# Scores of an RWKV-7 head pair in quadrants, and three steps around them in another order

## The chip, the core and the metric

The kernel runs on one core of a Trainium2 chip. The metric is the device time of one execution in microseconds. Three runs of the kernel before gave 1024.72 us as median (1024.06 to 1024.76).

Engines are called PE (TensorE, matmuls), DVE (VectorE), ACT (ScalarE), POOL (GpSimd) and SP (SyncE, which issues most loads). Each works through its own list of instructions in order; semaphores make one wait for another.

## The reference

One layer of a hybrid model on 512 tokens of width 1024: an RWKV-7 time mix with 16 heads of 64, a window attention, gates, a projection, and a feed-forward part with a short convolution. The change lies in the time mix:

```python
def step(S, inp):
    r_t, w_t, k_t, v_t, aa_t, bb_t = inp
    sa = jnp.einsum('bhvk,bhk->bhv', S, aa_t)
    S = S * w_t[:, :, None, :] + sa[..., None] * bb_t[:, :, None, :] + v_t[..., None] * k_t[:, :, None, :]
    y_t = jnp.einsum('bhvk,bhk->bhv', S, r_t)
    return S, y_t
...
y = (y - mean) * lax.rsqrt(var + GN_EPS)
y = y.reshape(B, T, RWKV_DIM) * lnx_w.astype(f32) + lnx_b.astype(f32)
bonus = jnp.sum(rh * kh * r_k.astype(f32), axis=-1, keepdims=True) * vh
y = (y + bonus.reshape(B, T, RWKV_DIM)) * g.astype(f32)
```

## The kernel before

The 512 steps of the recurrence are done in NT = 4 chunks of C = 128 tokens. Heads are taken in PAIRS = 8 pairs; the two heads of a pair lie on partitions 0 to 63 and 64 to 127. For each pair n, DVE prepares four operands: bp and kp (keys, all 512 tokens) and, in the tile ar, a-tilde and r-tilde side by side (2 x 128 columns a chunk). From them the kernel makes, per chunk and head, two triangular score matrices of 128 keys by 2 x 128 tokens: gb from bp, gk from kp. A key counts only for later tokens (a-tilde's half: strictly later; r-tilde's half: also the same one). The mask `causal` says so, and what it masks stays at the zero that POOL wrote once (and gb's -1 on the diagonal).

The part of a pair on PE is scores(n), then invert(n), then scan(n):

- scores(n, d), with d = n - 1. It waits for ops_ready (bp, kp and ar are there). Line L2291 makes 16 products: weights are 64 x 128 of bp or kp (one head, one chunk), 256 columns of ar move. Each fills half a PSUM bank; SCORE_BANK = (0, 1, 2, 3, 4, 5, 0, 1) gives the bank of each of eight halves of work f, so that f = 6 and 7 use the banks of 0 and 1 again and wait for two masked copies (g_ready). Then norm_var(d), L2226: the sums for the variance of the previous pair and the bonus sums, in four strips of 32 columns. Then turnings (transposes, L2232 and L2277): z (the values), bp, kp, and for the previous pair yrow (its standard deviation) and ysq (its reciprocal spread out).
- invert(n): a triangular inverse in LEVELS = 7 levels. At level 0 PE multiplies n1 (gb's first half, rounded to fp16 by ACT; n2 is the remainder, made by POOL at L738) by the identity (L2355); DVE masks the result to yy (L1597); from level 1 on PE makes L2351, DVE masks v (L1597), PE makes L2374, DVE adds to yy (L1608), ACT copies transposes. xx is made by DVE at L1582 from n1.
- scan(n): four chunks in turn, state, output.

Between these small steps PE always has "fill" work: L2046 to L2048, three products of 512 columns for one step of an unrelated big projection. The tables FILL and FILL_FIRST say how many such steps stand at each place ("scores", "centred", "tokens", (level, "masks") and so on).

DVE masks with copy_predicated (L1532, function masked), eight times a pair, 512 elements a partition each: f = 0 to 3 give gb, 4 to 7 give gk. In front of each stands a tiny memset of carrier. In pairs 1 to 7 deviations(d) (reciprocal L1520 and spread L1507) stands between the sixth and the seventh, and value_tokens(n) (L1497, L1499: the values less their mean) behind the eighth. Before the masks DVE splits weights (L1357) and, in pairs 1 and 2, also shifts a tile (L1392).

POOL, for each pair n > 0: bonus_product (L745), a copy (L752), remainder(n) (n2, L738), bonus_back(n - 1) (L814 writes the bonus rows to HBM once the deviation is there, L817 reads them back to all partitions), key_norms_in (L808), and the product of bonus and value (L850), which DVE uses at level 4. POOL also clears gb and, later, gk (L829) once before pair 0; the semaphore `cleared` counts 1, 2, 3 for gb, gk and zp.

SP's loads and their order are not touched.

## Time and profile before

| | |
|---|---|
| median of 3 runs | 1024.72 us (1024.06 to 1024.76) |
| profiled execution | 1024.05 us, of which the span of the trace is 1022.3 us |
| PE busy | 1011.7 us, 99% |
| DVE busy | 738.1 us, 72% |
| ACT busy | 516.2 us, 50% |
| POOL busy | 224.4 us, 22% |
| granted clock of PE | 0.999 of full speed |

The scores of pair 0 start at 213.64 us of the span, those of pair 7 at 498.12 us. Times in the rows are microseconds from the span's start. In the timeline views a row merges equal instructions that follow each other: it gives the start of the first, the time from there to the end of the last, and their number. Ends of matmuls are modelled and overlap the next one's start, so starts are compared with starts. An fp32 product on PE is two matmul instructions in these views; a turning (transpose) is one.

### The profile page before, as it was taken

The numbers are of one execution on the slowest core, as the hardware profiler recorded it, in microseconds if no ns is written. First come the engines' busy times: TensorE is split into PE (matmuls) and PEld (weight loads), VectorE is DVE, ScalarE is ACT, GpSimd is POOL, SyncE is SP. The second block draws the span as 40 slices with busy tenths as digits, with TensorE's granted clock in tenths as the row PEclk, the third lists the DMA queues.
The fourth block names the chain that finished last, engine by engine and source line by source line (L and its number), as shares of the span: only waits on it lengthen the run. The fifth ranks groups of instructions, "written<-read, shape, count | busy, mean of one in ns | idle before, by whom it ended". The sixth has DMA issues, their size and how long they took to land.

```text
span 1022.3 us, 18746 instructions
## 1 busy us (share of the span) xinstructions
PE 1011.7 (99%) x7106; PEld 806.3 (79%) x7106; DVE 738.1 (72%) x1233; ACT 516.2 (50%) x869; POOL 224.4 (22%) x298
## 2 busy tenths in 40 slices
PE   8999999999999999999999999999999999999997
PEld 7888888777777777777777888888888888888886
DVE  5224667788988888888877565367767777789786
ACT  6435756844435445345453322264455444467744
POOL 7642355330221422413210554000000000000000
PEclk9999999999999999999999999999999999999999
DMA  6874456331303313214255867613233333337662
GB/s 187 233 236 153 132 191 215 94 76 43 86 25 74 86 63 87 61 60 120 93 164 153 238 234 258 198 40 103 85 102 92 95 100 103 92 114 226 203 189 113
DMA packets 161291, 133.25 MB, mean 130 GB/s; under 512 B 32729, under 2 KB 137735, under 8 KB 161223
## 3 DMA queue, kind: packets, MB, share of 16 engines
q1 hardware_dynamic: 147687, 88.41, 29.7%
q0 software_dynamic: 13520, 43.90, 13.9%
q8 instruction: 47, 0.77, 0.3%
q14 instruction: 21, 0.17, 0.0%
q10 hardware_dynamic: 16, 0.00, 0.0%
HBM read 111.83 MB, written 20.45 MB: 129 GB/s over the span
## 4 chain that ended last, share of the span: by engine, by line
PE 94%; DVE 2%; DMA 1%; issue 1%; ACT 1%; POOL 0%; SPq 0%; DVEq 0%; POOLq 0%; ACTq 0%
PE ps L2090 14%; PE ps L2093 14%; PE ps L2092 14%; PE ps L2046 6%; PE ps L2048 5%; PE ps L2047 5%; PE ps L2677 3%; PE ps L2678 3%; PE ps L2679 3%; PE ps L2291 3%; PE ps L2425 2%; PE ps L2232 2%; PE ps L2613 1%; PE ps L2611 1%; PE ps L2612 1%; PE ps L2374 1%
## 5 line engine op out<-in xcount | busy, mean ns | idle before, releaser
L1357 DVE TENSOR_TENSOR wlo<-raw,whi 128x1024 fp32r<-128x1024 f32 x106 | 140.1, 1322 | 125.9 <-ACT whi L893 108.0
L893 ACT ACTIVATE whi<-raw 128x1024 fp32r<-128x1024 f32 x116 | 122.6, 1057 | 127.0 <-PE ps L2093 116.0
L2090 PE MATMUL ps<-xnh,whi 128*128 128x512 f32 x336 | 130.7, 389 | 0.0
L2092 PE MATMUL ps<-xnl,whi 128*128 128x512 f32 x336 | 130.7, 389 | 0.0
L2093 PE MATMUL ps<-xnh,wlo 128*128 128x512 f32 x336 | 130.7, 389 | 0.0
L2046 PE MATMUL ps<-xh,whi 128*128 128x512 f32 x192 | 89.5, 466 | 0.0
L2090 PE MATMUL ps<-xh,whi 128*128 128x512 f32 x224 | 88.3, 394 | 0.0
L2092 PE MATMUL ps<-xl,whi 128*128 128x512 f32 x224 | 87.3, 390 | 0.0
L2093 PE MATMUL ps<-xh,wlo 128*128 128x512 f32 x224 | 87.2, 389 | 0.0
L2048 PE MATMUL ps<-xh,wlo 128*128 128x512 f32 x192 | 76.1, 396 | 0.0
L2047 PE MATMUL ps<-xl,whi 128*128 128x512 f32 x192 | 75.3, 392 | 0.0
L2090 PEld LDWEIGHTS ps<-xnh,whi 128*128 128x128 f32 x336 | 63.1, 188 | 13.2
L2092 PEld LDWEIGHTS ps<-xnl,whi 128*128 128x128 f32 x336 | 63.1, 188 | 13.2
L2093 PEld LDWEIGHTS ps<-xnh,wlo 128*128 128x128 f32 x336 | 63.1, 188 | 13.0
L1093 ACT ACTIVATE xx<-ps 128x256 f16<-128x256 f32 x96 | 32.1, 381 | 69.1 <-PE ps L2331 68.3
L2090 PEld LDWEIGHTS ps<-xh,whi 128*128 128x128 f32 x224 | 42.0, 188 | 10.1 <-issue 0.8
L2093 PEld LDWEIGHTS ps<-xh,wlo 128*128 128x128 f32 x224 | 42.1, 188 | 8.9
L2092 PEld LDWEIGHTS ps<-xl,whi 128*128 128x128 f32 x224 | 42.1, 188 | 8.4
L1879 DVE TENSOR_TENSOR sq<-ps,rs 128x512 f32<-128x512 f32 x44 | 30.4, 691 | 23.5 <-PE ps L2093 18.5
L745 POOL TENSOR_TENSOR z<-z,kmod 128x512 f32<-128x512 f32 x8 | 16.2, 2025 | 126.2 <-DVE kp L1488 126.2
L2048 PEld LDWEIGHTS ps<-xh,wlo 128*128 128x128 f32 x192 | 36.0, 188 | 8.3
L1608 DVE TENSOR_TENSOR yy<-ps,yy 128x256 f16<-128x256 f32 x96 | 36.2, 419 | 8.6 <-PE ps L2374 8.3
(430 smaller groups left out, 2454.6 us busy)
## 6 DMA issues: line engine op xcount, KB each, us to landing
raw<-in_w_in SPq DMA_DIRECT2D x108, 256.0 KB, 3.3
raw<-in_w_up SPq DMA_DIRECT2D x88, 256.0 KB, 3.0
wrow<-in_w_down POOLq DMA_DIRECT2D x22, 512.0 KB, 5.1
raw<-weight_scratch SPq DMA_DIRECT2D x44, 256.0 KB, 3.4
raw<-in_w_down SPq DMA_DIRECT2D x32, 256.0 KB, 2.9
weight_scratch<-wrow POOLq DMA_DIRECT2D x11, 512.0 KB, 3.1
gates_scratch<-gst POOLq DMA_DIRECT2D x16, 256.0 KB, 3.2
raw<-in_w_proj_b SPq DMA_DIRECT2D x16, 256.0 KB, 4.2
```

The source lines that it names most:

```text
L893: act.activation(flat(whi[:, hb]), flat(raw[:, b]), ACT.Copy).then_inc(w_hi, 1)
L1093: act.activation(dst, src, ACT.Copy).then_inc(x_ready, 1)
L1357: dve.tensor_tensor(flat(lo[:, hb]), flat(raw[:, b]), flat(hi[:, hb]).bitcast(F32), ALU.subtract).then_inc(w_lo, 1)
L1608: dve.tensor_tensor(yg, low_half(ps[2 * g][:, :], lv), yg, ALU.add)\
L2046: pe.matmul(o, whi[:, hb, k, :], self.hi(k), start=k == 0, stop=False)
L2047: pe.matmul(o, whi[:, hb, k, :], self.lo(k), start=False, stop=False)
L2048: ins = pe.matmul(o, wlo[:, hb, k, :], self.hi(k), start=False, stop=k == KT - 1)
L2090: pe.matmul(ps[bank][:, :], whi[:, hb, k, :], hi(k), start=first and k == 0, stop=False)
L2092: pe.matmul(ps[bank][:, :], whi[:, hb, k, :], lo(k), start=False, stop=False)
L2093: ins = pe.matmul(ps[bank][:, :], wlo[:, hb, k, :], hi(k), start=False, stop=last and k == kn - 1)
L2291: ins = pe.matmul(ps[SCORE_BANK[f + h]][:, (j - j0) * 2 * C: (j - j0 + 1) * 2 * C], src[hs, j * C:(j + 1) * C], ar[hs, 1 - n % 2, j, :], s ...
L2677: pe.matmul(o, h_hi, hi[:, cols], start=start, stop=False)
```

## The change

It does four things.

1. Scores in quadrants. A chunk's 128 keys are split: the first 64 keys are multiplied with the first 64 tokens ("early", 64 x 64 weights, 2 x 64 = 128 columns, both chunks of a couple into the two partition halves of a bank), and all 128 keys with the last 64 tokens ("late", 128 columns). The last 64 keys with the first 64 tokens, all masked, are not computed. Early work goes to banks 2 and 3, late work of bp to 0 and 1, of kp to 4 and 5, so no bank is used twice and PE's wait inside the scores is gone.
2. The masked copies follow: four early ones on 64 partitions, each for gb and gk together (gb and gk become the two halves of a tile gg), two late ones for gb, two for gk. All four early ones wait for g_ps 4; in pair 0 they also wait for cleared 2, where the first copy waited for cleared 1. Memsets go from eight to five.
3. On DVE value_tokens and deviations stand between the sixth and seventh copy. On PE turned_var stands behind bp's turning, and turning ysq (deviations) and the wait for n1_ready stand behind the "tokens" fill of invert. Waits of g_ready change from 3, 4 and 8 to 2, 4 and 6, and ACT's copy to n1 waits for 6 instead of 4.
4. On POOL bonus_back stands before remainder, and remainder also waits for x_start, which DVE gives when xx is made.

```diff
--- before.py
+++ after.py
@@ -52,7 +52,8 @@
 RKV_TILES = 17
 RKV_LOOP = RKV_TILES - 1
 FILL_BANK = (7, 4, 7)
-SCORE_BANK = (0, 1, 2, 3, 4, 5, 0, 1)
+EARLY_BANK = (2, 3)
+LATE_BANK = ((0, 1), (4, 5))
 WARM = 24
 HALF_EXP = float(-0.5 * np.exp(-0.5))
 NEG = -1e30
@@ -273,11 +274,12 @@
         brow = take("brow", [P, P])
         lih = take("lih", [P, T], F32R)
         take = taker(KVR, PREP)
-        gb = take("gb", [P, NT, 2, 2 * C])
+        gg = take("gg", [P, NT, 2, 2, 2, C])
+        gb, gk = (gg[:, 2 * i:2 * i + 2].rearrange("p x e h q t -> p (x e) h (q t)")
+                  for i in range(2))
         gst = take("gst", [P, 2, T])
         xx = take("xx", [P, NT, 2, C], F16)
         ysb = take("ysb", [P, T])
-        gk = take("gk", [P, NT, 2, 2 * C])
         rkcols = take("rkcols", [P, P // NT])
 
 
@@ -735,6 +737,7 @@
 
             def remainder(n):
                 pool.wait_ge(n1_ready, n + 1)
+                pool.wait_ge(x_start, n + 1)
                 pool.tensor_tensor(n2[:, :, :, :], gb[:, :, :, 0:C], n1[:, :, :, :], ALU.subtract)\
                     .then_inc(n2_ready, 1)
 
@@ -841,8 +844,8 @@
                 if 3 * n - 1 >= FILL_V:
                     gate_out(3 * n - 1 - FILL_V)
                 odd_columns(n)
+                bonus_back(n - 1)
                 remainder(n)
-                bonus_back(n - 1)
                 if n < PAIRS - 1:
                     pool.wait_ge(rstd_ps, n)
                     key_norms_in(n + 1)
@@ -1069,7 +1072,7 @@
                 act.activation(flat(ktok), ps[1][:, :], ACT.Copy).then_inc(tok_ready, 1)
 
             def score_copy(n):
-                act.wait_ge(g_ready, n * 8 + 4)
+                act.wait_ge(g_ready, n * 8 + 6)
                 act.activation(n1[:, :, :, :], gb[:, :, :, 0:C], ACT.Copy).then_inc(n1_ready, 1)
 
             def hi_part(dst, src, i):
@@ -1520,19 +1523,42 @@
                 chain(dve.reciprocal(by_token(ystd[:, :]), by_token(ps[6][:, P:2 * P])))
                 spread(ysq, ystd).then_inc(vex_ready, 1)
 
-            def masked(n, f):
-
-                j0, h = (f % 4) // 2 * 2, f % 2
-                dst = (gb, gk)[f // 4][:, j0:j0 + 2, h, :]
+            def two_parts(t, ts):
+                return t.rearrange("p (q t) -> p q t", q=2)[:, :, ts]
+
+            def predicated(dst, mask, scores, f=None):
+                if f is not None:
+                    dve.memset(carrier[:, f:f + 1], 0.0)
+                dve.copy_predicated(dst, mask.bitcast(U32).unsqueeze(1)
+                                    .to_broadcast([mask.shape[0], NT, 2, C // 2]), scores)\
+                    .then_inc(g_ready, 1)
+
+            def late_masked(n, i, h):
+                f = 4 + 2 * i + h
                 if n == 0:
-                    dve.wait_ge(cleared, 1 + f // 4)
+                    dve.wait_ge(cleared, 1 + i)
                 dve.wait_ge(g_ps, n * 8 + f + 1)
-
-                dve.memset(carrier[:, f:f + 1], 0.0)
-                dve.copy_predicated(dst, causal[:, :].bitcast(U32).unsqueeze(1)
-                                    .to_broadcast([P, 2, 2 * C]),
-                                    ps[SCORE_BANK[f]][:, :].rearrange("p (j t) -> p j t", j=2))\
-                    .then_inc(g_ready, 1)
+                predicated((gb, gk)[i][:, :, h, :].rearrange("p j (q t) -> p j q t", q=2)
+                           [:, :, :, C // 2:], two_parts(causal[:, :], slice(C // 2, C)),
+                           ps[LATE_BANK[i][h]][:, :].rearrange("p (j q t) -> p j q t", j=NT, q=2), f)
+
+            def early_masked(n, h, e):
+                if n == 0:
+                    dve.wait_ge(cleared, 2)
+                dve.wait_ge(g_ps, n * 8 + 4)
+                predicated(gg[0:HD, :, e, h, :, 0:C // 2],
+                           two_parts(causal[0:HD, :], slice(0, C // 2)),
+                           ps[EARLY_BANK[h]][e * HD:(e + 1) * HD, :]
+                           .rearrange("p (x q t) -> p x q t", x=NT, q=2),
+                           None if h or e else 0)
+
+            def masked(n, i):
+                if i == 0:
+                    for h in range(2):
+                        for e in range(2):
+                            early_masked(n, h, e)
+                for h in range(2):
+                    late_masked(n, i, h)
 
             def add_bonus(d):
                 dve.wait_ge(bonus_ps, 1)
@@ -1714,9 +1740,9 @@
                 piece()
             attention_copy(7)
             weights(n + 2)
-            for f in range(8):
-                masked(0, f)
+            masked(0, 0)
             value_tokens(0)
+            masked(0, 1)
             invert(0, None, True)
             for n in range(1, PAIRS):
                 key, rates, factor, modified, removed, a_tilde, r_tilde, b_hat, k_hat = prepare(n)
@@ -1725,12 +1751,10 @@
                              (2, "s"): [r_tilde], (3, "z"): [b_hat], (3, "u"): [k_hat]})
                 weights(N_FILL + 3 * n)
                 fill_low(3 * n - 1)
-                for f in range(6):
-                    masked(n, f)
+                masked(n, 0)
+                value_tokens(n)
                 deviations(n - 1)
-                for f in range(6, 8):
-                    masked(n, f)
-                value_tokens(n)
+                masked(n, 1)
                 invert(n, n - 1, n < PAIRS - 1)
 
             def gated_bonus(d):
@@ -2281,32 +2305,47 @@
                 pe.wait_ge(ops_ready, n + 1)
                 if n == 0:
                     pe.wait_ge(ps_free, N_FILL - 1)
-                for f in range(0, 8, 2):
-                    src, j0 = (bp, kp)[f // 4], f % 4
-                    if f == 6:
-                        pe.wait_ge(g_ready, n * 8 + 2)
-                    for j in range(j0, j0 + 2):
-                        for h in range(2):
-                            hs = slice(h * HD, (h + 1) * HD)
-                            ins = pe.matmul(ps[SCORE_BANK[f + h]][:, (j - j0) * 2 * C:
-                                                                  (j - j0 + 1) * 2 * C],
-                                            src[hs, j * C:(j + 1) * C], ar[hs, 1 - n % 2, j, :],
+                rows = [slice(h * HD, (h + 1) * HD) for h in range(2)]
+
+                def both(hs, j, ts):
+                    return ar[hs, 1 - n % 2, j, :].rearrange("p (q t) -> p q t", q=2)[:, :, ts]
+
+                def late(i):
+                    src = (bp, kp)[i]
+                    for j in range(NT):
+                        for h, hs in enumerate(rows):
+                            ins = pe.matmul(ps[LATE_BANK[i][h]][:, j * C:(j + 1) * C]
+                                            .rearrange("p (q t) -> p q t", q=2),
+                                            src[hs, j * C:(j + 1) * C], both(hs, j, slice(HD, C)),
                                             start=True, stop=True)
-                            if j > j0:
+                            if j == NT - 1:
                                 ins.then_inc(g_ps, 1)
+
+                for i, src in enumerate((bp, kp)):
+                    for jj in range(2):
+                        o = (2 * i + jj) * C
+                        for e in range(2):
+                            j = 2 * jj + e
+                            for h, hs in enumerate(rows):
+                                ins = pe.matmul(ps[EARLY_BANK[h]][e * HD:(e + 1) * HD, o:o + C]
+                                                .rearrange("p (q t) -> p q t", q=2),
+                                                src[hs, j * C:j * C + HD], both(hs, j, slice(0, HD)),
+                                                start=True, stop=True)
+                                if i and jj:
+                                    ins.then_inc(g_ps, 1)
+                late(0)
+                late(1)
                 if d is not None:
                     norm_var(d)
                 fill("scores")
-                if d is not None:
-                    turned_var(d)
-                pe.wait_ge(g_ready, n * 8 + 3)
+                pe.wait_ge(g_ready, n * 8 + 2)
                 turned(2, z[:, n + 16, :]).then_inc(tok_ps, 1)
                 pe.wait_ge(g_ready, n * 8 + 4)
                 turned(3, bp).then_inc(tok_ps, 1)
                 if d is not None:
-                    deviations(d)
+                    turned_var(d)
                 fill("centred")
-                pe.wait_ge(g_ready, n * 8 + 8)
+                pe.wait_ge(g_ready, n * 8 + 6)
                 turned(1, kp).then_inc(tok_ps, 1)
 
             halves = [slice(h * HD, (h + 1) * HD) for h in range(2)]
@@ -2331,13 +2370,15 @@
                         ins = pe.matmul(o, yy[:, j, h, :], i, start=True, stop=True)
                     return ins
 
-                pe.wait_ge(n1_ready, n + 1)
                 for lv in range(LEVELS):
 
                     if lv == 4 and d is not None:
                         gate(d)
                     if lv == 0:
                         fill("tokens")
+                        if d is not None:
+                            deviations(d)
+                        pe.wait_ge(n1_ready, n + 1)
                     for g in range(2):
                         if lv == 0:
                             if g == 1:
```

PE in pair 1, before. The place begins at the scores and ends at the first matmuls of the inversion; fill work (L2046 to L2048) and the variance sums (L2226) are left out:

```order
L2291 MATMUL ps<-ar,bp 128x256 x8
L2291 MATMUL ps<-ar,kp 128x256 x8
...
L2277 MATMUL ps<-ident,yrow 128x128
L2232 MATMUL ps<-ident,z 128x128 x4
L2232 MATMUL ps<-ident,bp 128x128 x4
L2232 MATMUL ps<-ident,ysq 128x128 x4
...
L2232 MATMUL ps<-ident,kp 128x128 x4
...
L2355 MATMUL ps<-ident,n_95 128x64 x8
```

PE at the same place, after. L2330 are the early products, L2317 the late ones, L2256 and L2301 the turnings, L2396 the inversion's first matmuls:

```order
L2330 MATMUL ps<-ar,bp 64x128 x8
L2330 MATMUL ps<-ar,kp 64x128 x8
L2317 MATMUL ps<-ar,bp 128x128 x8
L2317 MATMUL ps<-ar,kp 128x128 x8
...
L2256 MATMUL ps<-ident,z 128x128 x4
L2256 MATMUL ps<-ident,bp 128x128 x4
L2301 MATMUL ps<-ident,yrow 128x128
...
L2256 MATMUL ps<-ident,kp 128x128 x4
...
L2256 MATMUL ps<-ident,ysq 128x128 x4
L2396 MATMUL ps<-ident,n_95 128x64 x8
```

Sixteen products of 256 columns have become 16 of 64 keys and 16 of 128 keys, each of 128 columns; yrow moved behind bp, and ysq from behind bp to behind kp.

DVE in pair 1, before, from the fifth masked copy to xx (the four before it are alike):

```order
L1532 COPY_PREDICATED gk<-causal,ps 128x2x256
L1531 MEMSET carrier 128x1
L1532 COPY_PREDICATED gk<-causal,ps 128x2x256
L1520 RECIPROCAL ystd<-ps 128x8
L1507 COPY ysq<-ystd 128x512
L1531 MEMSET carrier 128x1
L1532 COPY_PREDICATED gk<-causal,ps 128x2x256
L1531 MEMSET carrier 128x1
L1532 COPY_PREDICATED gk<-causal,ps 128x2x256
L1497 TENSOR_REDUCE vsum<-ps 128x8
L1499 SCALAR_TENSOR_TENSOR vp<-vsum,ps 128x512
L1582 TENSOR_TENSOR xx<-n_95,first_level 128x1024
```

DVE in pair 1, after, from the four early copies to the seventh; L1500 and L1502 are value_tokens, L1523 and L1510 deviations:

```order
L1532 COPY_PREDICATED gg<-causal,ps 64x4x2x64 x4
L1531 MEMSET carrier 128x1
L1532 COPY_PREDICATED gg<-causal,ps 128x4x2x64
L1531 MEMSET carrier 128x1
L1532 COPY_PREDICATED gg<-causal,ps 128x4x2x64
L1500 TENSOR_REDUCE vsum<-ps 128x8
L1502 SCALAR_TENSOR_TENSOR vp<-vsum,ps 128x512
L1523 RECIPROCAL ystd<-ps 128x8
L1510 COPY ysq<-ystd 128x512
L1531 MEMSET carrier 128x1
L1532 COPY_PREDICATED gg<-causal,ps 128x4x2x64
```

value_tokens has moved from behind the eighth copy to behind the sixth, in front of deviations.

POOL in pair 1, before, and then after (L741 is remainder, L817 and L820 the bonus rows, L811 the key rows):

```order
L745 TENSOR_TENSOR z<-z,kmod 128x512
L752 COPY yy<-ident 128x512
L738 TENSOR_TENSOR n_97<-gb,n_95 128x1024
L814 DMA bonus_scratch<-brow 128x128
L817 DMA z<-bonus_scratch 64x4x128 x2
L808 DMA kqn<-key_scratch 64x4x128 x2
L850 TENSOR_TENSOR z<-z 128x512
```

```order
L748 TENSOR_TENSOR z<-z,kmod 128x512
L755 COPY yy<-ident 128x512
L817 DMA bonus_scratch<-brow 128x128
L820 DMA z<-bonus_scratch 64x4x128 x2
L741 TENSOR_TENSOR n_97<-gg,n_95 128x1024
L811 DMA kqn<-key_scratch 64x4x128 x2
L853 TENSOR_TENSOR z<-z 128x512
```

Here n2 has moved behind the bonus rows' three DMAs.

## Rows read from the trace of the kernel before

**Rows 1.** The page's part 1: busy us (share of the span) and instructions of each engine

```profile
PE 1011.7 (99%) x7106; PEld 806.3 (79%) x7106; DVE 738.1 (72%) x1233; ACT 516.2 (50%) x869; POOL 224.4 (22%) x298
```

**Rows 2.** PE in order of time, pair 7; start us, length us, engine, line, operation

```profile
498.12 2.00 PE L2291 MATMUL ps<-ar,bp 64*128 64x256 f32 x16
...
501.78 0.43 PE L2226 MATMUL ps<-ysq,meancols 128*32 128x128 f32 x8
502.03 0.40 PE L2226 MATMUL ps<-z,rkcols 128*32 128x128 f32 x8
...
503.71 0.60 PE L2232 MATMUL ps<-ident,bp 128*128 128x128 f32 x4
504.19 0.66 PE L2232 MATMUL ps<-ident,ysq 128*128 128x128 f32 x4
...
504.92 0.40 PE L2047 MATMUL ps<-xl,whi 128*128 128x512 f32 x1
505.16 0.40 PE L2048 MATMUL ps<-xh,wlo 128*128 128x512 f32 x1
505.52 0.66 PE L2232 MATMUL ps<-ident,kp 128*128 128x128 f32 x4
...
508.63 0.42 PE L2351 MATMUL ps<-yy,n 128*128 128x64 f16 x8
```

**Rows 3.** PE in order of time, pair 1

```profile
253.87 2.00 PE L2291 MATMUL ps<-ar,bp 64*128 64x256 f32 x16
...
257.82 0.42 PE L2226 MATMUL ps<-ysq,meancols 128*32 128x128 f32 x8
```

**Rows 4.** DVE in order of time, pair 7; in brackets idle time before and what ended it

```profile
499.30 0.74 DVE L1532 COPY_PREDICATED gb<-causal,ps 128x512 f32<-128x512 uint32 x1 [0.29 <-issue]
...
499.93 0.73 DVE L1532 COPY_PREDICATED gb<-causal,ps 128x512 f32<-128x512 uint32 x1
...
503.47 0.21 DVE L1520 RECIPROCAL ystd<-ps 128x8 f32<-128x8 f32 x1 [0.24 <-PE ps L2277]
...
505.36 0.68 DVE L1497 TENSOR_REDUCE vsum<-ps 128x8 f32<-128x512 f32 x1
...
506.67 0.68 DVE L1582 TENSOR_TENSOR xx<-n,first_level 128x1024 f16<-128x1024 f16 x1
507.27 0.77 DVE L1597 TENSOR_TENSOR yy<-ps,level_mask 128x256 f16<-128x256 f32 x2
```

**Rows 5.** PE in order of time, scores of an attention window

```profile
84.36 1.16 PE L2176 MATMUL ps<-kb,qc 64*128 64x128 f32 x16
85.45 0.50 PE L2090 MATMUL ps<-xh,whi 128*128 128x512 f32 x1
```

**Rows 6.** PE in order of time, pair 0

```profile
218.51 0.60 PE L2232 MATMUL ps<-ident,z 128*128 128x128 f32 x4
...
223.84 0.44 PE L2351 MATMUL ps<-yy,n 128*128 128x64 f16 x8
```

**Rows 7.** DVE in order of time, pair 0

```profile
215.24 0.73 DVE L1532 COPY_PREDICATED gb<-causal,ps 128x512 f32<-128x512 uint32 x1
...
221.67 1.49 DVE L1582 TENSOR_TENSOR xx<-n,first_level 128x1024 f16<-128x1024 f16 x1
```

**Rows 8.** POOL in order of time, pair 0

```profile
215.26 1.88 POOL L829 MEMSET gk<- 128x2048 f32 x1
...
220.43 2.17 POOL L738 TENSOR_TENSOR n<-gb,n 128x1024 f16<-128x1024 f32 x1
```

**Rows 9.** One line, L1597; lengths in ns min/median/max, first and last start us

```profile
L1597 DVE TENSOR_TENSOR v<-ps,level_mask x96: 414/418/425, 224.2 to 521.9; 128x256 f16<-128x256 f32 x96
```

**Rows 10.** POOL in order of time, pair 7

```profile
506.15 0.57 POOL L814 DMA_DIRECT2D bonus_scratch<-brow  x1
...
514.66 1.29 POOL L850 TENSOR_TENSOR z<-z 128x512 f32<-128x512 f32 x1 [4.08 <-DMA z<-bonus_scratch]
```

**Rows 11.** DVE in order of time, pair 7, inversion's level 2

```profile
512.96 0.68 DVE L1569 TENSOR_TENSOR wlo<-raw,whi 128x512 fp32r<-128x512 f32 x1
```

## The prediction

> **What bounds the kernel now.** I read the page first: TensorE (PE) is busy 99% of the span [rows 1]. A microsecond cut from PE's own instructions is therefore gained, as long as nothing that PE waits for comes later than PE then arrives. I then read PE in order of time in the last pair of heads (n = 7), by starts: an instruction counts as busy until its modelled end, so busy time hides short stalls. The score matmuls run from 498.12 to 501.78 us, 3.66 us for 32 matmul instructions of 256 columns (each fp32 product is two instructions). From their start to the first L2351, the level-1 matmuls of the inversion, it is 508.63 - 498.12 = 10.51 us [rows 2]. Pair 1 takes 257.82 - 253.87 = 3.95 us for the same scores, since its last quarter waits for the masked copy that frees bank 0 [rows 3]. Then VectorE (DVE) over the same stretch: the eight masked copies follow each other every 0.63 us, with one hole of 0.24 us before the reciprocal, and DVE starts the first yy at 507.27, 1.36 us before PE's L2351 [rows 4]. One yy takes about 0.4 us, half of the 0.77 us of the two. What is left of these 1.36 us decides how much of a PE saving arrives.
>
> **PE's scores, pairs 1 to 7.** Before: 16 products of 64x128 weights with 256 columns. The two heads use different row halves and overlap: 3.66 us for 16 pairs of instructions. After: 16 products of all 128 keys with 128 columns ("late"), and 16 of 64 keys with 128 columns ("early"), which sit in four quadrants of the array. The late form exists in the trace: kb,qc, 64*128 weights and 128 columns, takes 85.45 - 84.36 = 1.09 us for 16 instructions, getting in and out included [rows 5]. If getting in and out is 0.2 of that, the 32 late ones take 2 x 0.9 + 0.2 = 2.0 us. No 64x64 quadrant runs in before. Nearest is ysq,meancols, four column strips at once: 8 instructions of 128 columns in 502.03 - 501.78 = 0.25 us [rows 2]; the 32 early ones at that rate take 1.0 us. The other end is two at a time, as kb,qc: 1.8 us. I take 1.0, since both forms show different parts of the array overlapping. Between early and late the tiles change shape once more: 0.1 us, half of what I gave kb,qc. New total 3.1 us. That is 0.56 less in pairs 3 to 7, and 0.85 less in pairs 1 and 2, because no bank is used twice any more.
>
> **PE's turnings.** Turning ysq stands behind bp's, and PE arrives before its operand: bp's four take 0.48 us until ysq starts, and ysq's are 0.66 us long where bp's are 0.60; 0.1 us is waiting. kp's start 0.36 us behind the filler's last start, where filler instructions follow each other at 0.24, and are 0.66 long too: 0.2 us of waiting, for the eighth masked copy [rows 2]. After the change kp waits for the sixth copy and ysq stands a filler block behind kp, so both waits should go: 0.3 us. PE's saving is 0.87 us in each of pairs 3 to 7 and 1.15 in 1 and 2.
>
> **Does DVE arrive in time?** Its work stays: eight copies of 512 elements a partition (four of them on 64 partitions, which I count as no cheaper), three memsets fewer, and the hole of 0.24 us goes because value_tokens now fills it. Its first copy can start where it did: the early products are done 1.3 us after the scores' start, and DVE came 1.18 us after it, from the weights [rows 2, 4]. From 499.30: six copies 3.7 us; reciprocal, spread and two copies 505.36 - 503.47 = 1.9; reduce, subtraction and xx 507.27 - 505.36 = 1.9 [rows 4]. The first yy starts near 506.8 and is ready near 507.3. PE arrives at 508.63 - 0.87 = 507.76: 0.4 us of slack. In pairs 1 and 2 DVE has one operation more (L1392) in front of its copies, so there I expect hardly any slack, and count 1.1 instead of 1.15. n1 waits for six copies instead of four, which moves ACT's copy by the time of one or two of them, not past xx. PE's wait for vex_ready now stands in front of the inversion's first matmuls; by the same counting the spread ends near 505.2 and PE is there at 505.4: no stall, but little room.
>
> **Pair 0 loses.** An early copy writes both gb and gk, so DVE's first one now waits until POOL has cleared gk. POOL does that from 215.26 to 217.14; DVE's first copy started at 215.24 [rows 6 to 8]. So DVE starts 1.95 us later, and its second copy is ready near 217.2 + 0.63 + 0.74 = 218.6. PE came to z's turning at 218.51 and, with shorter scores, would come at about 217.6: 1.0 us of standing. Its next turning, bp's, waits for the fourth copy, ready near 219.85, where PE is at 219.05; it starts near 219.95. From z's start to L2351 it was 5.33 us before, with z's four turnings, 0.44 us, ahead of bp's; so L2351 comes at 219.95 + 4.9 = 224.9 instead of 223.84 [rows 6]: a loss of 1.1 us. If POOL's clearing were hidden it would be nothing; the other end is the whole 1.95.
>
> **POOL.** The bonus rows go out before n2 is made, and n2 now waits for x_start; it is needed only at the end of the inversion. In pair 0 xx took 1.49 us, with POOL's n2 (220.43, 2.17 us) beside it, and 0.60 elsewhere [rows 4, 7, 8]. That goes, but PE, later itself in this pair, gains nothing from it. The Trainium skill, page "SBUF — State Buffer", section "SBUF: two separate sides", says that a VectorE operation with two SBUF inputs and a GpSimd operation that reads SBUF lock each other out of a shared port for the whole instruction. By that rule xx waited for n2's end at 222.60, and the trace agrees: it ended at 223.16.
>
> **The sum.** Pairs 3 to 7: 5 x 0.87 = 4.35. Pairs 1 and 2: 2 x 1.1 = 2.2. Pair 0: -1.1. Together 5.4 us less. The profiled execution took 1024.05 us (span 1022.3), so 1018.6; the median of the runs stands 0.7 above it, so 1019.3 us. After the pairs the same instructions follow behind the same PE, so nothing should give it back.
>
> **Rivals.**
> DVE becomes the bound of the stretch. For it: slack 0.4 us or less, and copies of 64-element runs that before does not have. Against: L1597's masks take 0.41 to 0.43 us in all 96 cases, at runs of every power of two from 1 to 64 [rows 9]. If every copy took 0.1 us more, eight of them are 0.8 us; less the slack, the pairs gain about 0.45: 7 x 0.45 - 1.1 = 2.0, 1022.7 us.
> Quadrants overlap only in part. With two at a time the early part takes 1.8 us: the scores come to 3.9, 0.25 more than now in pairs 3 to 7 against 0.3 from the waits that go; pairs 1 and 2 gain 0.35; pair 0 loses 1.1: 1024.4 us. Half way between, 1.4 us, each pair loses 0.4 of its gain: 1022.1 us. The Trainium skill, "TensorE: Matmul & The Clock Gate", section "Measured speedup vs the span model", has 3.07-fold for four row tiles, short of four; by it as an estimate the time would be 1020.7.
> The slower side: POOL's product of the bonus (L850) comes upon DVE's weights. In pair 7 it started at 514.66, 8.51 us behind the first bonus DMA (506.15), clear of the second L1569 (512.96) [rows 10, 11]. That DMA now goes out when ACT's root is done, by my estimate 4.4 us after the scores' start, 502.5. The product then runs from 511.0 to 512.3, and L1569 comes at 512.96 - 0.87 = 512.1: they touch by 0.2 us. A product that starts between 510.8 and 512.1 holds L1569 up, by at most its 1.29 us, and with it the level-3 masks behind it, for which PE waits. With 1.0 us in each of seven pairs: 1019.3 + 7 = 1026.3 us. For it: that closeness, and xx in pair 0, which lost 0.8 us in this way. Against: pair 7's DMA queue also brings q back, so the other pairs should have more room.
>
> **Chances.** Forecast 0.55; DVE as the bound 0.17; quadrants half way or by the page 0.10; two at a time 0.08; POOL's collision 0.10. A measurement of this kernel tells about 0.2% (2 us) from no change, so faster is below 1022.7: the forecast, the part-way case and half of the DVE case, 0.74. The other half of it and two at a time are the same, 0.16. Slower 0.10. The range reaches from 1018.0 (no cost for the change of tile shape, and 0.7 us less lost in pair 0) to 1023.6, past the DVE case and short of the last two.
>
> **What the profile after would show.** The 32 early instructions in about 1.0 us and the 32 late ones in 2.0; the first L2351 of pairs 3 to 7 some 9.65 us after the scores' start; no hole before DVE's reciprocal; masked copies still at 0.61 to 0.63 us; in pair 0 DVE's first copy at about 217.2, two PE waits behind it and L2351 11.3 us after the scores' start; xx there at 0.68 us; L850 clear of L1569. I am wrong if the early part takes over 1.4 us, if PE waits for yy at L2351, or if an L1569 or L1549 is much over 0.75 us.

## The result and the profile after

Before: 1024.46 us median of 20 runs (1023.90 to 1025.93). After: 1026.83 us median of 20 runs (1024.74 to 1028.87). The ratio is 1.0022, 95% interval 1.0015 to 1.0029: slower by 2.4 us, where 5.4 us less were forecast and the range ended at 1023.6. The runs also scatter more, over 4.1 us against 2.0. The profiled execution of the changed kernel took 1025.74 us, span 1024.0, so its profile shows about one microsecond less than the median loses.

The page's part 1 for the changed kernel (busy us, share of the span, instructions), to set beside [rows 1]:

```profile
PE 1008.4 (98%) x7362; PEld 808.6 (79%) x7362; DVE 736.0 (72%) x1209; ACT 516.3 (50%) x869; POOL 224.6 (22%) x298
```

PE is busy for 3.3 us less, and the span is 1.7 us longer: PE's work shrank, and PE stands more. TensorE in order of time, pair 7, answers to [rows 2]; columns are start us, length us, engine, line, operation, and in brackets the idle time before it with what ended it:

```profile
500.12 0.67 PE L2330 MATMUL ps<-ar,bp 64*64 64x128 f32 x16
...
501.16 1.16 PE L2317 MATMUL ps<-ar,bp 64*128 64x128 f32 x16
...
503.14 0.43 PE L2250 MATMUL ps<-ysq,meancols 128*32 128x128 f32 x8
...
507.10 0.40 PE L2072 MATMUL ps<-xh,wlo 128*128 128x512 f32 x1
507.79 0.66 PE L2256 MATMUL ps<-ident,ysq 128*128 128x128 f32 x4 [0.29 <-DVE ysq L1510]
...
510.18 0.53 PE L2392 MATMUL ps<-yy,n 128*128 128x64 f16 x8
```

The 32 early instructions take 501.16 - 500.12 = 1.04 us, the late ones 503.14 - 501.16 = 1.98, together 3.02 us where there were 3.66. But the first level-1 matmul (L2392, L2351 before) comes 10.06 us after the scores' start, not 9.64. Ahead of ysq's turning a start-to-start gap of 0.69 us stands where filler instructions follow each other every 0.24: 0.45 us of standing. The eight level-1 instructions themselves take 0.53 us where they took 0.42: in the trace's single records the fifth, the first that needs the second half of yy, starts 0.15 us behind the fourth, before 0.03. VectorE (DVE) in the same pair, beside [rows 4]:

```profile
501.38 0.72 DVE L1532 COPY_PREDICATED gg<-causal,ps 64x512 f32<-64x512 uint32 x1 [0.38 <-issue]
...
502.14 2.29 DVE L1532 COPY_PREDICATED gg<-causal,ps 64x512 f32<-64x512 uint32 x3
...
504.46 1.40 DVE L1532 COPY_PREDICATED gg<-causal,ps 128x512 f32<-128x512 uint32 x2
...
507.30 0.43 DVE L1510 COPY ysq<-ystd 128x512 f32<-128x512 f32 x1
...
509.52 0.77 DVE L1623 TENSOR_TENSOR yy<-ps,level_mask 128x256 f16<-128x256 f32 x2
```

The second copy starts 0.76 us behind the first, and the fifth 504.46 - 502.14 = 2.32 us behind the second, 0.77 each; before they came every 0.63. DVE has no idle time between copies and none before the reciprocal, and still reaches yy 8.14 us after its first copy, where it took 7.97 before and 7.5 was forecast. Pair 0, TensorE, beside [rows 6]:

```profile
219.58 0.66 PE L2256 MATMUL ps<-ident,z 128*128 128x128 f32 x4 [1.10 <-DVE gg L1532]
221.10 1.11 PE L2256 MATMUL ps<-ident,bp 128*128 128x128 f32 x4 [0.86 <-DVE gg L1532]
221.86 0.78 PE L2070 MATMUL ps<-xh,whi 128*128 128x512 f32 x1
222.44 0.63 PE L2071 MATMUL ps<-xl,whi 128*128 128x512 f32 x1
...
227.46 0.42 PE L2392 MATMUL ps<-yy,n 128*128 128x64 f16 x8
```

The two waits that were forecast are there, 1.10 and 0.86 us. Behind them is what was not: filler instructions follow each other every 0.42 to 0.58 us. The table by stretches shows why; its columns are PE, PEld, DVE, ACT and POOL busy, the granted clock, DMA share and GB/s:

```profile
217.50:219.50 2.00, 0.98 (x5) 0.49 (x3) 1.42 (x3) 0.00 (x0) 2.00 (x3) 1.00 0.88 243
219.50:220.50 1.00, 0.66 (x4) 0.42 (x4) 0.94 (x3) 0.00 (x0) 1.00 (x3) 1.00 0.23 71
220.50:221.00 0.50, 0.00 (x0) 0.00 (x0) 0.50 (x2) 0.00 (x0) 0.50 (x2) 0.75 0.00 0
221.00:222.00 1.00, 0.90 (x5) 0.91 (x5) 0.96 (x5) 0.00 (x0) 0.26 (x1) 0.50 0.67 49
222.00:223.00 1.00, 1.00 (x4) 0.81 (x4) 1.00 (x2) 0.53 (x1) 0.00 (x0) 0.50 0.90 53
223.00:224.00 1.00, 1.00 (x4) 0.81 (x3) 0.97 (x4) 0.94 (x2) 0.00 (x0) 0.50 0.51 94
224.00:225.00 1.00, 1.00 (x7) 0.80 (x7) 1.00 (x4) 1.00 (x2) 0.00 (x0) 0.92 0.24 66
```

PE was busy for 1.64 of the 3.5 us from 217.5 to 221.0, and then the granted clock is 0.50, the 1.2 GHz level, until about 224. The stretch from the scores to L2392 takes 227.46 - 214.50 = 12.96 us, 2.76 more than before and not 1.1. Last, GpSimd (POOL) and DVE in pair 5, around the second half of the weights' low part (L1595, L1569 before), beside [rows 10, 11]:

```profile
433.16 1.29 POOL L853 TENSOR_TENSOR z<-z 128x512 f32<-128x512 f32 x1 [1.06 <-DMA z<-bonus_scratch]
```

```profile
433.56 1.44 DVE L1595 TENSOR_TENSOR wlo<-raw,whi 128x512 fp32r<-128x512 f32 x1
```

POOL's product starts first and lasts until 434.45; DVE's subtraction, 0.68 us by itself, takes 1.44. POOL's product starts when a DMA has landed, 12.97 to 14.11 us after the scores' start in pairs 1 to 7 of this execution, and the subtraction starts at about 14.5 (14.7 and 14.8 in pairs 2 and 1). It is longer than 0.68 us in pair 5 (1.44) and in pair 6 (0.82); in x_memsets, below, an L1595 is longer in pairs 3, 4, 6 and 7. So whether they meet differs from pair to pair and from execution to execution.

### The profile page after: what moved, and what is told of

The parts are those of the page before. It is cut to its first block, busy times and chain, and to the rows that moved or that the text cites. A ratio compares the mean times of both kernels' runs of the same rounds, so it can differ in the third digit from the quotient of the medians.

```text
span 1024.0 us, 19242 instructions
## 1 busy us (share of the span) xinstructions
PE 1008.4 (98%) x7362; PEld 808.6 (79%) x7362; DVE 736.0 (72%) x1209; ACT 516.3 (50%) x869; POOL 224.6 (22%) x298
## 3 DMA queue, kind: packets, MB, share of 16 engines
q0 software_dynamic: 13520, 43.90, 14.7%
## 4 chain that ended last, share of the span: by engine, by line
PE 89%; DVE 7%; issue 2%; DMA 1%; ACT 0%; POOL 0%; DVEq 0%; POOLq 0%; ACTq 0%
PE ps L2114 14%; PE ps L2117 14%; PE ps L2116 14%; PE ps L2070 5%; PE ps L2072 4%; PE ps L2071 4%; PE ps L2718 3%; PE ps L2720 3%; PE ps L2719 3%; DVE gg L1532 2%; PE ps L2653 1%; PE ps L2654 1%; PE ps L2652 1%; PE ps L2392 1%; PE ps L2466 1%
## 5 line engine op out<-in xcount | busy, mean ns | idle before, releaser
L1532 DVE COPY_PREDICATED gg<-causal,ps 64x512 f32<-64x512 uint32 (+1 forms) x64 | 45.7, 738 | 4.8 <-issue 1.9
```

The costliest lines, as they stand in the source:

```text
L1532: dve.copy_predicated(dst, mask.bitcast(U32).unsqueeze(1) .to_broadcast([mask.shape[0], NT, 2, C // 2]), scores)\
```

## Experiments

Every run is the changed kernel but for the edits named; a line's number can be one or two off from it. Small differences between medians stay within the intervals, so the traces are read beside them. Before is near 1024.5 us in every comparison (1024.36 to 1024.63).

**1. A copy that waits for a copy, or a copy that changes the half it reads (x_memsets, x_order).** The early copies read PSUM partitions 0 to 63 (e = 0) and 64 to 127 (e = 1) in turn. The first edit gives every early copy the small memset that only the first had:

```
-                           None if h or e else 0)
+                           2 * h + e)
```

> The changed kernel with a memset of carrier put back in front of each of the four early masked copies (eight memsets again). In the trace after, early copies start 0.73 to 0.78 us apart instead of the 0.63 us of before, and PE stands about 0.45 us before turning ysq in each of pairs 1 to 7. Theory M (the copies are slow because the semaphore wait sits on the copy itself, with no memset in between to carry it): the early copies come 0.63 us apart, PE's wait for ysq shrinks to 0.1 us, and the time falls by 7 x 0.35 = 2.5 us. Theory Q (a copy is held until the one before it has finished when its source lies in the other partition half of the bank): the spacing stays at 0.73 us or more, and the time does not change by more than 0.5 us.

Measured 1025.82 us (1024.25 to 1028.29; ratio 1.0013, 1.0004 to 1.0023), and the copies still 0.76 to 0.78 us apart. What stands between them is not the cause. The second edit only changes their order, to e = 0, 0, 1, 1:

```
-                    for h in range(2):
-                        for e in range(2):
+                    for e in range(2):
+                        for h in range(2):
...
-                pe.wait_ge(g_ready, n * 8 + 2)
+                pe.wait_ge(g_ready, n * 8 + 3)
                 turned(2, z[:, n + 16, :]).then_inc(tok_ps, 1)
```

> The changed kernel with the four early masked copies in the order bank 2, bank 3 of the lower partition half, then bank 2, bank 3 of the upper half, still without memsets between them; z's turning then waits for three copies instead of two. Theory Q: the first to the second and the third to the fourth copy come 0.60 to 0.63 us apart, the second to the third still 0.73 or more; DVE is 0.25 us earlier, PE's wait for ysq in pairs 1 to 7 falls from 0.45 to about 0.2 us, and the time by 1.7 us. Theory M: all three spacings stay at 0.73 or more, and the time stays within 0.5 us, or is a little longer for z's later wait in pair 0.

Measured 1022.16 us (1021.12 to 1025.93; ratio 0.9982, 0.9971 to 0.9993). DVE in pair 7:

```profile
499.60 0.73 DVE L1532 COPY_PREDICATED gg<-causal,ps 64x512 f32<-64x512 uint32 x1 [0.38 <-issue]
...
500.24 2.09 DVE L1532 COPY_PREDICATED gg<-causal,ps 64x512 f32<-64x512 uint32 x3
...
502.37 1.38 DVE L1532 COPY_PREDICATED gg<-causal,ps 128x512 f32<-128x512 uint32 x2
```

From the first start to the second 0.64 us, from there to the fifth 2.13 in place of 2.32. Instruction by instruction the gaps are 0.64, 0.73, 0.64 and 0.76: only the two copies that read another half than the one before them are late. The bank is no rival: in this order every step changes it, and only two of the four are late, where in the changed kernel all four are, two of them within one bank. That confirms it by shape. The time (9 runs) fell by 4.7 us where 1.7 were expected, and the stretches of the profiled executions give 2.3; experiment 3 prices the order without collisions.

**2. The collision on POOL (x_product_late, x_product_hit, x_pool_undone).**

```
                 pool.wait_ge(bonus_in, 32 * n)
+                pool.wait_ge(w_lo, N_FILL + 3 * n + 2)
                 pool.tensor_tensor(z[:, n + 7, :], ...
```

> The changed kernel, but POOL's product of bonus and value also waits for DVE's second half of weights at level 2 (w_lo), so that it starts behind that L1595 and not in front of it. In the trace after, the product starts 0.3 us or less from colliding in most pairs, and in pairs 5 and 6 one L1595 takes 1.44 and 0.82 us instead of 0.68. Theory P (these collisions, with bonus rows that land at varying times, make the changed kernel's runs spread from 1024.7 to 1028.9 us and cost 1 to 2 us in the median): every L1595 is 0.68 us, the runs spread over less than 1.5 us, and the median falls by 1 to 2 us, to about 1025.3. Rival (the spread comes from elsewhere, as from the stop in pair 0): spread and median stay.

Measured 1024.13 us (1023.30 to 1024.72; ratio 0.9995, 0.9986 to 1.0004): 2.7 us less than the changed kernel, every L1595 (L1596 here) at 679 to 683 ns, and the runs 1.4 us apart in place of 4.1. Expected were 1 to 2 us. The counter-test makes them meet in every pair, with a wait for y_ready[0] of (LEVELS - 1) * n + 2 at the same place:

> The changed kernel with GpSimd's product of the bonus row held until the level-1 product of VectorE is through, so that it starts just ahead of the second half of the level-2 weights in every pair, and no longer at a time that the DMA of the bonus row sets. Theory P: that half takes 1000 to 1500 ns in place of 682 in pairs 1 to 7, each costs its excess, and the time is 1024.1 us plus seven times 0.5 to 0.8, 1027.6 to 1029.7 us. Rival (the long halves come from the DMAs of the key rows, not from the product): 680 to 690 ns in most pairs and about 1024 to 1026 us.

Measured 1029.78 us (1029.55 to 1030.64, 4 runs; ratio 1.0052, 1.0037 to 1.0066). POOL and DVE in pair 5:

```profile
436.19 1.28 POOL L854 TENSOR_TENSOR z<-z 128x512 f32<-128x512 f32 x1 [1.47 <-DVE yy L1635]
```

```profile
436.29 1.73 DVE L1596 TENSOR_TENSOR wlo<-raw,whi 128x512 fp32r<-128x512 f32 x1
```

The subtraction waits out the product and then takes its own time: 436.19 + 1.28 + 0.68 = 438.15, measured end 438.02. It took 1724 to 1736 ns in all seven pairs, an excess of 1.05, of which the path felt (1029.78 - 1024.13) / 7 = 0.81 a pair. I had expected 0.5 to 0.8, and at most 1.5 us for the subtraction. The third undoes the change's order on POOL instead:

```
-                pool.wait_ge(x_start, n + 1)
...
-                bonus_back(n - 1)
                 remainder(n)
+                bonus_back(n - 1)
```

> The changed kernel with one part undone: GpSimd's order of before (the bonus row is read back ahead of the rest of the key rows' work, no wait for the next pair's start). Theory P (GpSimd's product beside VectorE's level-2 weights is what costs and scatters): the product goes back to about 15.8 us behind the start of the scores, all halves of the weights in pairs 1 to 7 take 680 to 690 ns, the spread of the runs falls under 2 us, and the time is 1024.1 us, as with the product held back by a wait. Rival: the order itself saved time elsewhere (xx in pair 0 was held 0.8 us in the kernel before), then xx in pair 0 takes about 1500 ns again and the time is 1025 us or more.

Measured 1042.45 us (1041.29 to 1043.22, 5 runs; ratio 1.0173, 1.0160 to 1.0186). The rival's signs came, over 1025 us and xx of pair 0 at 1.38, but neither theory had the cause of 15.6 us on top of the changed kernel's time. POOL and DVE in pair 5, then TensorE by stretches:

```profile
434.87 2.13 POOL L740 TENSOR_TENSOR n<-gg,n 128x1024 f16<-128x1024 f32 x1 [3.58 <-ACT n L1075]
```

```profile
435.13 2.14 DVE L1509 COPY ysq<-ystd 128x512 f32<-128x512 f32 x1
```

```profile
436.00:438.00 2.00, 0.67 (x8) 0.66 (x9) 2.00 (x5) 0.70 (x2) 1.50 (x2) 1.00 0.00 0
...
440.00:442.00 2.00, 2.00 (x13) 1.38 (x12) 0.76 (x2) 0.00 (x0) 1.52 (x3) 0.50 0.75 49
```

The early start of POOL's n2 now lies upon the spread of ysq, a copy of 0.43 us in the changed kernel, which takes 2.13 to 2.15 in all of pairs 1 to 7 here; TensorE stands 2 us for it. In pairs 2, 3, 5 and 7 the clock falls to 0.50 afterwards, and the stretch from the scores to level 1 takes 12.7 to 13.5 us; in pairs 1, 4 and 6 the clock stays at 1.00, and it takes 11.8 to 11.9. The edit undoes two things, the order and n2's wait for x_start, and tells only that together they keep n2 off the spread, which I had valued at nothing beyond pair 0. By the changed kernel's trace the order alone may do: the last of the bonus rows' DMA issues (L820), behind which n2 now stands, ends 0.3 to 2.1 us after the spread in every pair. In the kernel before the same two just missed each other, in the other order. Its pair 5, DVE and then POOL:

```profile
422.47 0.43 DVE L1507 COPY ysq<-ystd 128x512 f32<-128x512 f32 x1
```

```profile
422.82 2.15 POOL L738 TENSOR_TENSOR n<-gb,n 128x1024 f16<-128x1024 f32 x1 [2.65 <-ACT n L1073]
```

The spread had started 0.35 us ahead of n2 and took its 0.43.

**3. Pair 0, and the three edits together (x_clear_early, x_dummies, x_two, x_all).** POOL clears gk for pair 0 only behind its work on the attention output. The edit clears it ahead of the last part of that:

```
-            attention_out(7)
-            pool.wait_ge(ops_ready, 1)
+            pool.wait_ge(o_ps, 16)
             pool.memset(gk[:, :, :, :], 0.0).then_inc(cleared, 1)
+            attention_out(7)
```

> The changed kernel, but POOL clears gk as soon as the last attention values are out of PE (o_ps 16), in front of its store of the attention output, so that DVE's first masked copy of pair 0 need not wait for it. In the trace after, pair 0's stretch from the scores to L2392 takes 12.97 us against 10.21 before; about 1.3 us of the loss is PE standing and 1.4 us PE at half clock from 220.8 to 224.3 us of the span. Theory C (both follow from that one wait): the stretch takes 9.7 to 10.0 us, the clock stays full, and the time falls by 3 us, to about 1023.8. Rival (PE would stand behind the slower copies anyway): the stretch takes over 10.8 us and the gain is under 2 us.

Measured 1024.27 us (1021.86 to 1027.48; ratio 1.0005, 0.9996 to 1.0014), 2.6 us less. The profiled execution, the fastest of the 11, has TensorE in pair 0:

```profile
213.92 0.67 PE L2330 MATMUL ps<-ar,bp 64*64 64x128 f32 x16 [0.71 <-DVE kp L1491]
...
218.62 0.66 PE L2256 MATMUL ps<-ident,bp 128*128 128x128 f32 x4 [0.26 <-DVE gg L1532]
...
223.67 0.52 PE L2392 MATMUL ps<-yy,n 128*128 128x64 f16 x5
```

The stretch is 9.75 us, below the 10.21 of the kernel before, and the clock stays at 1.00. How much of the loss is standing and how much is the clock, the next run tells. It keeps the late clearing, holds the product back as x_product_late does, and lets TensorE turn the identity where it would stand:

```
+                if n == 0:
+                    pe.wait_ge(o_done, 8)
+                    for _ in range(11):
+                        pe.transpose(ps[7][:, 0:P], ident[:, :], ident[:, :])
                 pe.wait_ge(g_ready, n * 8 + 2)
...
+                if n == 0:
+                    for _ in range(9):
+                        pe.transpose(ps[7][:, 0:P], ident[:, :], ident[:, :])
                 pe.wait_ge(g_ready, n * 8 + 4)
```

> The kernel with the product held back (1024.13 us), and in pair 0 alone 20 turnings of the identity on TensorE that nobody reads, 11 ahead of its wait for the turning of z and 9 ahead of its wait for that of bp: work without use, in the place of standing. It tells two parts of pair 0's loss apart. Theory K (TensorE stands in pair 0, then the granted clock falls to 0.5 and costs as much again as the standing): the clock stays at 1.0 through pair 0, the stretch from the first score to the level-1 matmul falls from 13.1 to about 11.7 us, and the time to 1022.7 us. Rival (the clock falls for another reason, or the stretch is bound by VectorE's copies whatever the clock): 13.1 us and 1024.1 us.

Measured 1023.41 us (1022.92 to 1023.96; ratio 0.9990, 0.9981 to 0.9999). TensorE in pair 0, then by stretches:

```profile
217.54 1.36 PE L2345 MATMUL ps<-ident 128*128 128x128 f32 x11
218.85 0.66 PE L2257 MATMUL ps<-ident,z 128*128 128x128 f32 x4
219.35 1.15 PE L2350 MATMUL ps<-ident 128*128 128x128 f32 x9
```

```profile
221.00:222.00 1.00, 1.00 (x6) 0.81 (x5) 1.00 (x4) 0.22 (x1) 0.00 (x0) 1.00 1.19 66
222.00:223.00 1.00, 1.00 (x8) 0.83 (x8) 0.96 (x4) 1.00 (x2) 0.00 (x0) 1.00 0.57 90
```

With useless work in the same place the clock stays full, and the stretch is 11.7 us as expected, against 13.13 in x_product_late. x_memsets, with the late clearing and no dummies, has the same two waits in pair 0. TensorE, and the 3.5 us that answer to 217.5 to 221.0 above:

```profile
218.71 0.66 PE L2256 MATMUL ps<-ident,z 128*128 128x128 f32 x4 [1.11 <-DVE gg L1532]
220.23 0.66 PE L2256 MATMUL ps<-ident,bp 128*128 128x128 f32 x4 [0.87 <-DVE gg L1532]
...
225.26 0.61 PE L2392 MATMUL ps<-yy,n 128*128 128x64 f16 x8
```

```profile
216.62:220.12 3.50, 1.64 (x9) 0.90 (x7) 2.85 (x8) 0.00 (x0) 3.50 (x6) 1.00 0.58 160
```

TensorE is busy for the same 1.64 us, and yet there the granted clock stays at 1.00 behind it, and the stretch is 225.26 - 213.62 = 11.64 us. So the low clock costs 1.3 to 1.4 us where it comes, the standing and the later copies the other 1.4, and the same waits bring it in one execution and not in another. That the dummies keep the clock up is therefore likely, but one profiled execution doesn't show it. The medians differ by 0.7 only, the profiled executions by 1.3 (1024.72 and 1023.41): the profiled one of x_product_late was the slowest of its 11. How often the clock falls in the unprofiled executions stays open.

Two edits together, with the copies in the changed kernel's order, and then all three:

> The changed kernel with two of the three edits, gk cleared early and GpSimd's product held back, and the masked copies in the changed kernel's own order. Beside the run with all three (1018.95 us) it prices the order of the copies alone, with no collision in either. Theory Q (a copy whose source lies in the other partition half than the last one's is held for 0.12 to 0.15 us; five such changes in place of two before the sixth copy): stretch to the level-1 matmul 10.05 us in pairs 4 to 7 against 9.72, and 1021.5 us. Rival (the order is worth what its own run showed, 4.7 us, through something else than the stretch): 1023.5 us.

Measured 1021.60 us (1021.15 to 1024.13; ratio 0.9980, 0.9971 to 0.9989), stretches 10.04 to 10.06 us in pairs 3 to 7. The two edits add: 1026.83 less 2.6 and 2.7 is 1021.5. The mean granted clock is 0.997 in the three executions from 1023.99 to 1024.13 us, and 0.999 or 1.000 in the eight from 1021.15 to 1023.36: also without pair 0's waits a low clock comes in some.

> The changed kernel with three edits together: GpSimd clears gk before it works on the last values of the part ahead of pair 0, GpSimd's product of the bonus row waits until VectorE's second half of the level-2 weights is done, and the masked copies go through one partition half of the score bank after the other. Theory: the three losses are separate, so their effects add. From the changed kernel's 1026.8 us: the clear took off 2.6, the product 2.7, the order 4.7 with its collisions still in. With the collisions counted once, 1018.4 us (1017.4 to 1019.6); from the start of the scores to the level-1 matmul 9.4 to 9.8 us in pair 0, 9.7 to 9.8 us in pairs 4 to 7; every half of the weights 680 to 690 ns; granted clock 1.0 in pair 0. Rival: they hide one another (what is won before the level-1 matmul is stood out behind it, on the bonus rows' way through memory), then it stays above 1021 us.

Measured 1018.95 us (1018.62 to 1023.80, 6 runs; ratio to before 0.9955, 0.9941 to 0.9970). TensorE in pair 7:

```profile
494.52 0.67 PE L2331 MATMUL ps<-ar,bp 64*64 64x128 f32 x16
...
501.50 0.40 PE L2073 MATMUL ps<-xh,wlo 128*128 128x512 f32 x1
501.85 0.66 PE L2257 MATMUL ps<-ident,ysq 128*128 128x128 f32 x4
...
504.25 0.53 PE L2393 MATMUL ps<-yy,n 128*128 128x64 f16 x8
```

504.25 - 494.52 = 9.73 us; the gap ahead of ysq is down from 0.69 to 0.35. The order of the copies alone is worth 1021.60 - 1018.95 = 2.65 us, which is what the stretches of all eight pairs give, 0.26 to 0.42 each and 2.6 together. (The expectation counted five changes of half; the starts show four, against two.) The 2.0 us more that x_order gained on the changed kernel may come from fewer or shorter collisions or from the scatter, since each median is known to about 1 us; that was not shown apart. This version beats both kernels, by 5.5 us the one before.

**4. Where the stretch is bound (x_swap, x_best).** In pairs 1 to 7 the norm's division goes ahead of the value sums, once beside the late product and once beside all three edits:

```
-                value_tokens(n)
                 deviations(n - 1)
+                value_tokens(n)
```

> The kernel with the product held back (1024.13 us), and in VectorE's order of pairs 1 to 7 the division of the norm (reciprocal and spread) ahead of the value sums, not behind them. VectorE's work up to the first yy is the same; only ysq is ready 1.35 us earlier. Theory S (TensorE stands only ahead of turning ysq, about 0.45 us; the first yy, ready at 9.78 us, is then the next thing to be late): no gap at ysq, the level-1 matmul at 9.8 instead of 10.05 us, and 1024.1 less seven times 0.25, 1022.4 us. Rival (VectorE's whole chain bounds the stretch, so that TensorE stands at the level-1 matmul instead): 10.05 us and 1024.1 us.

> The kernel with all three edits (1018.95 us) and the norm's division ahead of the value sums too. There TensorE's gap ahead of turning ysq is 0.35 us where filler instructions follow each other every 0.24, so 0.1 us is waiting in each of pairs 1 to 7, and the first yy is ready 0.25 us before TensorE comes to the level-1 matmul. Theory S: 9.63 us in pairs 4 to 7, and 1018.3 us. Rival (nothing left to gain there): 9.72 us and 1018.95 us.

x_swap: 1023.21 us (1022.97 to 1024.53; ratio 0.9989, 0.9980 to 0.9998). ysq's turning has no wait any more, 7.22 us after the scores' start instead of 7.65, and yet the level-1 matmul comes at 9.96, between the two theories, 0.09 earlier and not 0.25; the time fell by 0.9, within the intervals. TensorE in pair 7:

```profile
508.88 0.61 PE L2393 MATMUL ps<-yy,n 128*128 128x64 f16 x8 [0.28 <-DVE yy L1624]
```

From yy's start to it there are 0.58 us, in place of 0.67; in no run here were there fewer. The eight instructions now take 0.61 us, with 0.24 us between the fourth and the fifth: both halves of them start 0.14 us behind the end of the half of yy that they read. So VectorE's whole chain bounds the stretch, and the standing only moves. x_best lost, though the two intervals overlap: 1020.51 us (1020.23 to 1023.77, 5 runs; ratio 0.9965, 0.9951 to 0.9978), 1.6 above x_all. DVE in pair 6:

```profile
462.05 1.40 DVE L1533 COPY_PREDICATED gg<-causal,ps 128x512 f32<-128x512 uint32 x2
...
463.59 0.21 DVE L1524 RECIPROCAL ystd<-ps 128x8 f32<-128x8 f32 x1
```

The second of the two copies starts at 462.70 and a following instruction could start at about 463.31; the reciprocal starts at 463.59, since its input, turned by TensorE, is not there: 0.28 us of hole, on an engine that is the bound. In pairs 3 to 7 the stretch is 9.92 to 9.94 in place of 9.71 to 9.74; pairs 1 and 2 have no such hole and keep theirs (9.94 and 9.93, in place of 9.96 and 9.99). 5 x 0.2 is 1.0 us; 0.4 more lie behind the level-1 matmul's start, since the fifth instruction waits as in x_swap. The profiled execution of x_best was the slowest of its 5 (1023.77): TensorE stood 2.5 us ahead of pair 0's scores, the clock fell to 0.50, and that pair took 10.72 us.

## Why the prediction was wrong

What held. The scores on TensorE: 3.02 us against 3.1, the early part 1.04 against 1.0, all four quadrants overlapping. Both rivals on quadrants fall. (By its own terms the one with two at a time comes to 1024.9 us, not 1024.4: it loses 0.15 on the kernel before.) The waits of pair 0 were in their places; xx there took 0.67 us; the first copy of a pair started 1.26 us behind the scores.

Three steps failed. Their prices, from different runs, add to 7.6 us, where 7.5 lie between 1019.3 and 1026.8. That they agree so well is partly luck: pair 0's price holds for an execution in which the clock falls, and 0.8 us more, told below, belong to none of the three.

**"It stays" of DVE's work (3.3 us).** I took six copies to follow every 0.62, 3.7 us in all. They take 4.4: a copy whose source starts in the other partition half of PSUM comes 0.73 to 0.78 us behind the last one (0.80 in a few cases), not 0.63. With the changed kernel's order of loops four of the first five steps from copy to copy change the half, where one half read to its end needs two. The first yy thus started 9.40 us after the scores, in pair 7, and not 8.68, which is past the slack of 0.4: pairs 1 to 7 gained 0.41 to 0.55 us each, 3.3 in all, against 6.55. x_all beside x_two gives the order 2.3 us of what is missing; the other 0.95 is missing in x_all too, which still changes the half twice, and no run takes it apart. That is the rival "DVE becomes the bound", which I priced at 0.45 a pair and gave 0.17. My argument against it, that L1597's lengths don't depend on their runs [rows 9], spoke of how an element is reached, and the cost was in what the instruction before had read. The Trainium skill, "VectorE: DVE Perf Modes", section "Two Vector instructions with no wait between them", has this rule, as a model: a Vector instruction whose input starts in another quadrant than the last one read from the same memory starts only when every earlier one has finished. By that rule exactly the copies at a change are late, whatever memset stands between, and both runs of experiment 1 agree; what it costs, 0.10 to 0.15 us a change for these copies, is from the runs, and would have put the time into the rival's.

**"A loss of 1.1 us" in pair 0 (1.7 us).** The loss is 2.76. The mechanism was right and its price lacked the clock: 1.3 us of it are the granted clock of 0.50, which followed the two waits in this execution and not in x_memsets, where the loss is 1.43 us. The 0.3 us that are left over the forecast lie, by argument only, with the slower copies, which I had counted at 0.63 here too.

**"They touch by 0.2 us" (2.7 us).** The collision of POOL's product with the subtraction was the rival on the slower side, with 0.10. Its place and mechanism were right: x_product_late takes 2.7 us off, x_product_hit adds 0.8 a pair. It was not 7 pairs of 7 (two in the changed kernel's trace), and it came with DVE 0.5 us later than forecast. My own estimate of the start, 511.0 in pair 7, lay inside the window in which I said it hurts, 510.8 to 512.1, and yet the sum charged nothing for it, not even the 0.2 us of touching. A start that scatters by over a microsecond beside a window of that width should have been charged in part to every case. The range left it out.

**"Nothing should give it back" (0.8 us).** From the first level-1 matmul to the next pair's scores TensorE needs 30.22 us in pairs 1 to 4 where it needed 30.07 to 30.11, and 30.18 to 30.24 in x_product_late, where nothing collides. The fifth level-1 instruction's wait of 0.12 us for the second half of yy accounts for it. So TensorE does wait for yy at level 1, which the prediction had named as a sign of being wrong.

A further step cost nothing here but was misread: the new order on POOL was counted as worth nothing beyond pair 0. x_pool_undone shows that without it and n2's wait for x_start the changed kernel takes 1042.45 us. The Trainium skill's rule of the shared port ("SBUF — State Buffer", section "SBUF: two separate sides"), which I used for xx alone, counts an fp32 copy from SBUF to SBUF among the operations that take the port, and so bears on the spread of ysq as well. By that rule the spread waits for n2's end: the trace agrees, 2.14 us beside a POOL subtraction of 2.13.

## What to carry to other kernels

When an output is split over quadrants of the array, ask what the engine that evacuates it pays: let it read one partition half to the end before it goes to the other. When work on an engine is moved, lay every GpSimd operation beside each VectorE operation between SBUF tensors, and where a DMA sets the start, charge the collision by the width of its scatter or fix the start with a wait. A wait on the bounding engine may cost more than its length: look at the granted clock behind it, in more than one execution, and prefer to move the cause (here a memset) rather than to fill the hole.

## What the runs showed of the hardware

- Sixteen products of 64x64 weights and 128 columns in four quadrants take 1.04 us for 32 instructions; in two row halves of 64x128 weights 32 instructions take 1.98.
- A masked copy of 64 partitions takes as long as one of 128: starts 0.63 us apart in x_order and in the kernel before.
- A DVE operation between SBUF tensors that comes upon a running POOL operation between SBUF tensors waits until that ends: 1.73 us in place of 0.68 beside POOL's product, 2.14 in place of 0.43 beside its subtraction n2.
- In x_memsets one such subtraction, in pair 3, took 2.59 us: it started 0.75 us ahead of POOL's product, while POOL issued DMAs, and ended 0.55 us behind it. Why POOL had its turn first is open.
- PE busy for 1.64 of 3.5 us was followed by 3.4 us at a granted clock of 0.50 (1.2 GHz) in the changed kernel, and by none in x_memsets with the same two waits; stands of 2 us in x_pool_undone were in four pairs of seven. The waits of 0.45 us in pairs 1 to 7 were not.
